# A hybrid decoder layer on one Trainium2 core: keys and queries transposed in squares by VectorE and over DRAM, the taps of a block redistributed, the first products' order and one sum changed

## The reference, cut to what matters

```python
z = h @ w_in                                   # 2048 -> 12288 columns: q, k, v, u, ga and gc, 2048 each
q, k, v, u, ga, gc = jnp.split(z, list(np.cumsum(IN_SPLITS)[:-1]), axis=-1)
# 16 heads of 128: scores = q k^T * scale - slope * distance, causal, softmax, times v
y_attn = o.transpose(0, 2, 1, 3).reshape(B, S, ATTN_WIDTH) @ w_attn_out
# u: a * sigmoid(g), a depthwise convolution with 31 taps over 1024 channels, norm, silu, product
merged = jax.nn.sigmoid(ga) * y_attn + jax.nn.sigmoid(gc) * y_conv
return merged @ w_out
```

## Time and profile before

| | |
|---|---|
| time, median of 3 runs | 2117.32 us (2117.2 to 2117.87) |
| the profiled execution's own time | 2117.16 us |
| its span | 2115.3 us |
| TensorE busy | 2102.1 us (99%) |
| VectorE busy | 1868.6 us (88%) |
| ScalarE busy | 1406.2 us (66%) |
| POOL busy | 194.2 us (9%) |
| HBM | 529.93 MB read, 16.78 MB written |

### The profile page before, as it was taken

The page is one execution under the profiler, slowest core; times in us unless marked ns, Lnnn a source line. Parts: engine busy times, 40 slices in busy tenths (PEclk is TensorE's granted clock), DMA queues, the critical chain, the costliest instruction groups (busy, mean ns, idle before and its releaser), DMA issues.

```text
span 2115.3 us, 23794 instructions
## 1 busy us (share of the span) xinstructions
PE 2102.1 (99%) x9420; PEld 1740.6 (82%) x9420; DVE 1868.6 (88%) x1404; ACT 1406.2 (66%) x1321; POOL 194.2 (9%) x305
## 2 busy tenths in 40 slices
PE   9999999999999999999999999999999999999998
PEld 7888888888888888888888888888888888888886
DVE  8899999999997889999899986659899999999996
ACT  6677777778775547666676435435677777777773
POOL 0111111100110000000000000000111111110110
PEclk9999999999999999999999999999999999999999
DMA  9688888898886759787888656755688888898883
GB/s 359 238 285 274 266 268 269 293 308 277 288 276 237 274 154 316 251 261 224 273 266 251 232 189 231 259 187 199 237 289 262 276 262 275 290 308 276 288 276 123
DMA packets 89709, 548.26 MB, mean 259 GB/s; under 512 B 12416, under 2 KB 12800, under 8 KB 32512
## 3 DMA queue, kind: packets, MB, share of 16 engines
q1 hardware_dynamic: 68544, 437.69, 54.5%
q0 software_dynamic: 21056, 109.07, 24.5%
HBM read 529.93 MB, written 16.78 MB: 258 GB/s over the span
## 4 chain that ended last, share of the span: by engine, by line
PE 99%; DMA 0%; DVE 0%; SPq 0%; ACT 0%; issue 0%; DVEq 0%
PE acc L2194 16%; PE acc L2196 16%; PE acc L2195 16%; PE tb L2194 12%; PE tb L2196 12%; PE tb L2195 12%; PE acc L2132 3%; PE acc L2134 3%; PE acc L2133 3%; PE tb L2180 1%; DMA g_raw<-in_groups 0%; PE tb L2475 0%; PE tb L2491 0%; PE tb L2492 0%; PE tb L2474 0%; DVE res L2035 0%
## 5 line engine op out<-in xcount | busy, mean ns | idle before, releaser
L1326 DVE TENSOR_TENSOR g_lo<-g_raw,g_hi 128x2048 fp32r<-128x2048 f32 x506 | 1147.3, 2285 | 136.5 <-ACT g_hi L804 136.1
L804 ACT ACTIVATE g_hi<-g_raw 128x2048 fp32r<-128x2048 f32 x506 | 964.7, 1916 | 343.3 <-DVE g_raw L1334 105.4
L2194 PE MATMUL acc<-g_hi,xF_hi 128*128 128x512 f32 x1216 | 477.9, 393 | 1.9 <-DVE g_lo L1653 1.3
L2196 PE MATMUL acc<-g_hi,xF_lo 128*128 128x512 f32 x1216 | 473.7, 390 | 0.0
L2195 PE MATMUL acc<-g_lo,xF_hi 128*128 128x512 f32 x1216 | 473.2, 389 | 0.0
L2194 PE MATMUL tb<-g_hi,xF_hi 128*128 128x512 f32 x760 | 297.1, 391 | 0.0
L2196 PE MATMUL tb<-g_hi,xF_lo 128*128 128x512 f32 x760 | 295.9, 389 | 0.0
L2195 PE MATMUL tb<-g_lo,xF_hi 128*128 128x512 f32 x760 | 295.7, 389 | 0.0
L1334 DVE TENSOR_TENSOR g_raw<-g_raw,g_raw 128x2048 f32<-128x2048 f32 x120 | 274.3, 2286 | 1.4
L2194 PEld LDWEIGHTS acc<-g_hi,xF_hi 128*128 128x128 f32 x1216 | 228.3, 188 | 50.3 <-DVE g_lo L1653 2.6
L2196 PEld LDWEIGHTS acc<-g_hi,xF_lo 128*128 128x128 f32 x1216 | 228.3, 188 | 48.2
(11 more groups left out here) (169 smaller groups left out, 2243.5 us busy)
## 6 DMA issues: line engine op xcount, KB each, us to landing
g_raw<-in_groups SPq DMA_DIRECT2D x356, 1024.0 KB, 7.0
g_raw<-in_groups POOLq DMA_DIRECT2D x80, 1024.0 KB, 8.3
raw<-in_stream SPq DMA_DIRECT2D x80, 512.0 KB, 4.7
bounce<-h_sq POOLq DMA_DIRECT2D x40, 256.0 KB, 5.0
h_in<-bounce POOLq DMA_DIRECT2D x160, 64.0 KB, 2.8
ln_gb<-in_ln SPq DMA_DIRECT2D x6, 1024.0 KB, 6.9
g_raw<-in_groups SPq DMA_DIRECT2D x6, 512.0 KB, 9.1
res<-in_x_rows SPq DMA_DIRECT2D x1, 2048.0 KB, 16.0
```

Of the source, the lines that this page charges most:

```text
L804: act.activation(g_hi[:, n % RING], source[:], ACT.Copy).then_inc(g_hi_ready, 1)
L1326: dve.tensor_tensor(g_lo[:, n % RING], source[:], f32(g_hi[:, n % RING]), ALU.subtract).then_inc(g_lo_ready, 1)
L2194: pe.matmul(bank, x_hi_ap, g_hi[:, n % RING, blk], start=begin, stop=False, skip_group_check=True)
L2196: return pe.matmul(bank, x_lo_ap, g_hi[:, n % RING, blk], start=False, stop=end, skip_group_check=True)
```

## The change

Five edits:

1. The key and query transposes leave TensorE. VectorE transposes 32x32 squares of both (four passes per head block), POOL stores them to two new DRAM buffers and loads them back in 16 pieces, ScalarE copies the queries into `qT`; the keys are loaded straight into `kT`, in another order of the tokens' addresses, which the scores' products read with strides (`tokens`). ScalarE no longer copies keys.
2. TensorE makes the first pair's scores behind P5a (before: ahead of it) and the second pair's behind P6a (before: ahead of it).
3. `BLOCK_TAPS` has ten numbers per block. Head blocks have none in the first four places and 2 or 3 in the others; the gate chunks get one more per group.
4. In `first_chunk` TensorE runs the two kinds of products that need only `g_hi` first and those with `g_lo` behind them; `WARM` is 10.
5. In the first feed-forward part the sum T3 of block 1 is made by POOL's adding DMA, and two low halves of x factors (`factor_lo(f, 2)`, `(f, 3)`) move behind T1.

```diff
-WARM = 12
+WARM = 10
...
-BLOCK_TAPS = ((1, 3), (1, 3), (1, 3), (1, 3), (2, 3), (2, 1))
+HEAD_TAPS = (0, 0, 0, 0, 2, 2, 3, 3, 3, 3)
+BLOCK_TAPS = ((3, 3, 1, 1, 3, 1, 1, 1, 1, 1), *([HEAD_TAPS] * NG), (1, 1, 2, 2, 1, 2, 2, 2, 2, 2))
...
-            def heads_of(dst, g, first):
-
-                for t in range(TT):
-                    act.wait_ge(tr_full, turned(g) + first + t + 1)
-                    act.activation(dst[:, :, t * P:(t + 1) * P], tb[:, t].rearrange("p (b n) -> p b n", b=HG),
-                                   ACT.Copy).then_inc(qk_ready, 1)
...
             def queries_turned(g):
+
+                act.wait_ge(q_loaded, 16 * TT * QD * (g + 1))
                 if g:
                     act.wait_ge(o_stored, 16 * g)
-                heads_of(qT, g, 2)
+                for t in range(TT):
+                    act.activation(qT[:, :, t * P:(t + 1) * P].rearrange("p b (a n) -> p a b n", a=QD), q_sq[t][:],
+                                   ACT.Copy).then_inc(qT_ready, 1)
...
-                if heads:
-                    keys_turned(g - 1)
-                elif g == 0:
+                if g == 0:
                     conv_block(1)
                 fork(f, g, acc[:, BY], acc[:, BX], "P1b")
                 act.wait_ge(t1b_ready, fulls(f, g))
                 split(f, g, "P5b", "qb")
+                split_sum(f, g, "P6a", "qa", "T2a")
                 if heads:
                     queries_turned(g - 1)
-                split_sum(f, g, "P6a", "qa", "T2a")
...
-                load_done(f, b, "ua")
-                dve.wait_ge(t_ready, G.sum_no[f, b, "T1"])
-                add(ra, ra, ua)
+                if f:
...
+                else:
+                    factor_lo(f, 2)
+                    factor_lo(f, 3)
+                    load_done(f, b, "ua")
...
+            def square(dst, src, squared_one):
+
+                dve.transpose(dst.rearrange("p c b n -> p b c n"),
+                              src.rearrange("p (b c n) -> p b c n", b=BLK, c=QD)).then_inc(squared_one, 1)
...
                 lo_group(f, g, "P1b", "qb")
+                if heads:
+                    keys_squared(g - 1)
                 split_done(f, g, "P1a")
                 load_done(f, g, "ra")
                 add(qa, qa, ra)
                 lo_group(f, g, "Q1", "Q1")
...
-                taps(some)
+                if heads:
+                    queries_squared(g - 1)
+                taps(counts[0])
...
-                taps(5 if g - 1 in HEADS_AT else 7)
+                taps(6 if g - 1 in HEADS_AT else 8)
...
+            def squares_out(g, squared_one, squares, dram, sent):
+
+                for t in range(TT):
+                    pool.wait_ge(squared_one, 2 * g + t + 1)
+                    pool.dma_start(dram[t].rearrange("a p c b n -> (a p) (c b n)"),
+                                   squares[t].rearrange("p c b n -> p (c b n)")).then_inc(sent[t], 16)
+
+            def heads_in(g, sent, dst, dram, loaded_all):
+
+                for t in range(TT):
+                    pool.wait_ge(sent[t], 16 * (g + 1))
+                    for c in range(QD):
+                        pool.dma_start(dst[t][STEP * c:STEP * (c + 1)].rearrange("p a b n -> p a (b n)"),
+                                       dram[t, :, :, c].rearrange("a p b n -> p a (b n)")).then_inc(loaded_all, 16)
...
+            pool.wait_ge(t_ready, G.sum_no[0, 1, "T1"])
+            add_from_hbm(0, 1, "ra", "ua", t3_first)
             round_trips(0)
...
                 for h, (g, first, last) in enumerate(PARTS):
                     p = g // 2
-                    pe.wait_ge(part_lo, h + 1)
+                    pe.wait_ge(part_hi, h + 1)
...
+                    for t in range(TT):
+                        for blk in range(first, last):
+                            high_only(banks[g % 2][t], piece(p, t)[0][:, blk], g, blk, p == 0 and blk == 0)
...
+                    pe.wait_ge(part_lo, h + 1)
+                    for t in range(TT):
+                        for blk in range(first, last):
+                            mm = high_low(banks[g % 2][t], piece(p, t)[0][:, blk], g, blk)
...
-                if heads:
-                    turn_k(g - 1)
...
-                if heads:
-                    turn_q(g - 1)
                 query_group(g, 1)
-                if heads:
-                    scores(g - 1, 0)
...
                 product_group(f, g, "P5a", W, S1, 0, begin=True)
+                if heads:
+                    scores(g - 1, 0)
                 product_group(f, g, "P5b", W, S1, 1)
+                wait_fork(f, g, 0)
+                product_group(f, g, "P6a", X, S2, 0)
                 if heads:
                     scores(g - 1, 1)
-                wait_fork(f, g, 0)
-                product_group(f, g, "P6a", X, S2, 0)
```

More of the change, by code:

```diff
@@ L154, in __init__ @@
                     rows += 1
-                for name in FULL_SUMS if is_full(b) else HALF_SUMS:
+                for name in FULL_SUMS if is_full(b) else HALF_SUMS[f]:
                     sums += 1
@@ L431, in build @@
         t1b_ready = sem("t1b_ready")
+        t3_first = sem("t3_first")
         t3b_ready = sem("t3b_ready")
@@ L475, in build @@
         conv_step = sem("conv_step")
-        qk_ready = sem("qk_ready")
+        k_squared = sem("k_squared")
+        q_squared = sem("q_squared")
+        k_sent = [sem(f"k_sent{t}") for t in range(TT)]
+        q_sent = [sem(f"q_sent{t}") for t in range(TT)]
+        kT_loaded = sem("kT_loaded")
+        q_loaded = sem("q_loaded")
+        qT_ready = sem("qT_ready")
         s_ready = sem("s_ready")
@@ L1810, in mixing_block @@
                 qa, qb, ra, ua, ub = (source(f, g, name) for name in ("qa", "qb", "ra", "ua", "ub"))
-                few, some = BLOCK_TAPS[g]
+                counts = BLOCK_TAPS[g]
                 heads = 0 < g <= NG
@@ L1829, in mixing_block @@
                 add(qa, qa, ua)
-                taps(some)
+                taps(counts[1])
                 lo_group(f, g, "P5b", "qb")
@@ L1850, in mixing_block @@
                     normalised(g - 1)
-                taps(some)
+                taps(counts[4])
                 lo_group(f, g, "P4a", "qa")
-                taps(few)
+                taps(counts[5])
                 lo_group(f, g, "P2a", "ga")
-                taps(few)
+                taps(counts[6])
                 lo_group(f, g, "P2b", "gb")
-                taps(few)
+                taps(counts[7])
                 lo_group(f, g, "P4b", "qb")
-                taps(few)
+                taps(counts[8])
                 lo_group(f, g, "Q4", "Q4")
                 values(g)
-                taps(few)
+                taps(counts[9])
             taps_done = [0]
@@ L2100, in mixing_sums @@
                 add_from_hbm(f, g, "qb", "rb", t1b_ready)
+                if 0 < g <= NG:
+                    squares_out(g - 1, k_squared, [kT[:, t] for t in range(TT)], k_bounce, k_sent)
+                    squares_out(g - 1, q_squared, [tile[:] for tile in q_sq], q_bounce, q_sent)
+                    heads_in(g - 1, k_sent, [kT[:, t] for t in range(TT)], k_bounce, kT_loaded)
+                    heads_in(g - 1, q_sent, [tile[:] for tile in q_sq], q_bounce, q_loaded)
                 k = G.load_at[f, g, "rb"]
@@ L2244, in plain_chunk, with high_only, high_low @@
                                     after[(2 * p + half, t)]()
+            def high_only(bank, x_ap, n, blk, begin):
+                pe.matmul(bank, x_ap, g_hi[:, n % RING, blk], start=begin, stop=False, skip_group_check=True)
+            def high_low(bank, x_ap, n, blk):
+                return pe.matmul(bank, x_ap, g_lo[:, n % RING, blk], start=False, stop=False, skip_group_check=True)
             def first_chunk():
@@ L2253, in first_chunk @@
                     p = g // 2
-                    pe.wait_ge(part_lo, h + 1)
+                    pe.wait_ge(part_hi, h + 1)
+                    if h in (0, 4, 6):
+                        pe.wait_ge(x_hi, (0, 4, 6).index(h) + 1)
+                    for t in range(TT):
+                        for blk in range(first, last):
+                            high_only(banks[g % 2][t], piece(p, t)[0][:, blk], g, blk, p == 0 and blk == 0)
                     if h in (0, 4, 6):
@@ L2258, in first_chunk @@
                         for blk in range(first, last):
-                            mm = mm3(banks[g % 2][t], piece(p, t)[0][:, blk], piece(p, t)[1][:, blk], g, blk,
-                                     p == 0 and blk == 0, False)
+                            high_only(banks[g % 2][t], piece(p, t)[1][:, blk], g, blk, False)
+                    pe.wait_ge(part_lo, h + 1)
+                    for t in range(TT):
+                        for blk in range(first, last):
+                            mm = high_low(banks[g % 2][t], piece(p, t)[0][:, blk], g, blk)
                     if last == GK:
```

69 lines of the change are left out of this document (39 added, 30 removed).

## The result

| | before | changed |
|---|---|---|
| time, median of 4 runs | 2117.35 us (2117.20 to 2117.87) | 2150.66 us (2149.73 to 2152.24) |
| the profiled execution's own time | 2117.16 us | 2149.73 us |
| its span | 2115.3 us | 2147.9 us |
| TensorE busy | 2102.1 us | 2103.7 us |
| POOL busy | 194.2 us | 240.6 us |

The ratio is 1.0157, with an interval of 1.0141 to 1.0173: slower, by 33.3 us or 1.6%. The forecast was 2112.2, its range ended at 2126.0.

The account below looks back on a forecast made before the run. TensorE's list was taken to bound the kernel: 2117.16 - 7.0 (transposes) - 1.2 (first products) + 2.8 (trip over DRAM) + 0.4 (VectorE's squares) = 2112.2 us, range 2108.5 to 2126.

Parts of the forecast that it names:

- The way over DRAM: Head blocks: queries' trip by POOL and DMA ends 0.7 us after the scores are due, 2.8 us back over four blocks.
- I take the best rows: Trip over DRAM: choice of the profile's best stall and landing times, giving 0.7 us late per block.
- T1b's landing before the first load: Sign named for the head blocks: POOL's sum T1b lands before the first key load.
- the keys sent at +6.5: Trip's start: keys stored to DRAM 6.5 us after the block's first product; +7.9 at worst.
- The middling values: Trip over DRAM with 6.3 us for a lot and 2.8 to land: about 4.9 us late per block.
- Rival (b): Head blocks: the trip sets the block, 4.9 us late each, 19.6 back, 2129 us in all; chance 0.25.
- Transposes off TensorE: Head blocks: two lots of eight transposes at 0.87 us leave TensorE in four blocks, 7.0 us less.
- Squares on VectorE: Head blocks: four transposes, 2.6 to 2.8 us, fit on VectorE; no lead at P3b, 0.4 us in all.
- First products: Kernel's start: fifth part begins at about 12.4 instead of 13.63, 1.2 us less, and u1 without a wait.
- Taps: Nine more in each head block's second part, eight in the gate chunks: costs nothing, or 1 us if lead runs out.

Follow-up runs that it names:

- experiment 2: Changed kernel with 30 products of no use on TensorE ahead of each head block's first scores, in the gap of the wait: 2143.78 us.
- experiments 7 and 9: 7: changed kernel with the sum T1b cut to one row of 128 in the four head blocks, 2147.37 us; 9: the run act_loads, 2122.39 us.
- act_loads: Changed kernel with the queries' eight loads issued by ScalarE on its own queue instead of by POOL: 2122.39 us, ratio 1.0023.
- first_alone: Kernel before with edits 4 and 5 alone (first products, WARM, T3 by POOL), transposes staying on TensorE: 2116.35 us, ratio 0.9995.
- keys_final: Changed kernel, but queries transposed on TensorE; T3a before T3b in last head block, taps moved, attention rows sooner, third ones in two parts: 2111.98 us, ratio 0.9974.
- act_mended: act_loads with T3a ahead of T3b in the last head block, five taps per head block ahead of the second biases, attention rows sooner: 2120.42 us.
- experiment 4: Changed kernel with the gate chunks' taps as before and seven more taps in the last head block: 2149.19 us.
- k_trip_first: Changed kernel with the keys' stores and their eight loads all issued by POOL ahead of the sum T1b: 2158.71 us.

## Why the prediction was wrong

With what was measured, its own sum reads 2117.16 - 7.0 - 1.2 + 30.0 + 9.2 + 1.4 = 2149.6; the profiled execution took 2149.73. The 9.2 is what the blocks' lengths left over, so that the sum closes proves nothing by itself; experiment 2 is what ties it to the clock.

- **The way over DRAM failed, at "I take the best rows".** The forecast was 0.7 us late per block, the measured value 7.5. T1b's landing before the first load and the keys sent at +6.5 were right, and so were little over 2 us for the queries' loads, though these fell on +17.6 to +25 and not on +12 to +18. Wrong was the keys' lot: I took 0.91 us for its stall and had in mind the stretch from 845.70 with the DMA share at 0.14, where the queries' loads were to fall. (Even +12 to +18 was half outside it: from 842.80 to 848.80 the share was 0.43.) The keys' fell on +6 to +15, where the share was 0.98 before any edit. They landed in 7.1 us instead of 2.1, POOL stalled 6.8 us on them, and the queries' loads, quick in themselves, stood behind. The middling values, 4.9 us, were nearer, and they too were low.
- **A term was missing: the clock.** Each wait of 2.7 us and more was followed by products at the lower level; at 4.5 us and more it cost some 2 us each time, and even about 2 us of wait could do it. The sum priced a wait at its length, in every rival. Rival (b) was the one that came, with the right place and sign, and put 19.6 on it where 39.2 were measured.
- **The best value was chosen for a wait that all depends on.** The prediction itself said that three of its numbers were the best of their rows, and a rule of the Trainium skill (page "VectorE: DVE Perf Modes", section "Rules for kernel authors"), that such a transpose belongs on TensorE, stood against it. For the queries and keys together the rule held in every run; for the keys alone it did not, once the waits behind were mended. As to the cause, experiments 7 and 9 give the effect of each alone, which need not add: T1b's 1 MB 1 us a block, the queries' loads in POOL's queue 6. The Trainium skill, page "DMA: Bandwidth & Descriptors", section "Rules for kernel authors", says that spreading transfers over issuing engines adds no bandwidth and saves only issue time. The first half agrees (over a block's first 15 us the engines moved 298 GB/s with the loads on ScalarE's queue and 297 without). The time saved was no trifle here: 28.3 us, since with the issues went POOL's stalls and the place behind the keys.
- **Transposes off TensorE:** right. No run gives the 7.0 by itself, but in act_loads, where the clock stayed up, the first blocks took 66.9 us less their waits where they took 68.5 before, and for the keys alone the spans of first_alone and keys_final differ by 3.1 us where 3.5 is the sum, with the waits at both nearly alike.
- **Squares on VectorE:** right for the kernel as it is (no wait for a low half in the head blocks), and as tight as forecast: the five taps of act_mended made P3b 0.8 late.
- **First products:** right, 1.2 us in the trace of the changed kernel and between the medians of first_alone, whose interval still holds no change. In the other runs with this start P1a of the first head block began between 828.88 and 829.75, 1.0 to 1.9 us sooner than before. u1 had no wait.
- **Taps:** "nothing" was off by 1.4 us, at the output products, beyond the gate chunks where I had looked. Half of it is the taps; the other half stays open, behind a high half of ScalarE's (experiment 4).
- **Slips that changed nothing:** by its own terms the range up to 2126 takes in 4.2 us of lateness a block, not 3.4. The taps added to the second part of a head block are eight in three blocks and three in the last, not nine.

## What to carry to other kernels

A share or a landing time has to be read in the stretch where each transfer will fall, one stretch for every lot, since the lots of one queue add up. Where an engine that bounds the kernel may wait, price the wait at its length and add what its clock costs behind it; here the first 1.9 us cost no more than themselves, 5 us did. When a trip is late, try another engine's queue as well as another order, and halve the edit: here the half with the keys was in time and worth keeping.

## What had not been expected of the hardware

- POOL's issue of a load stalls, it seems while too much of what it has issued has not landed: one to four stalls per lot of 512 KB, in eight transfers or four, up to 6.7 us long (k_trip_first, last head block). A lot in a quiet stretch had one of 1.9 to 2.1 us. ScalarE's queue took the same eight with no stall, in 4.2 us. That it goes by what has not landed fits all of this and is not proven.
- TensorE's clock fell in waits of 4.5 us and more (0.50 behind one of 7.5), fell also in one of 2.7 (0.61 behind it) and in four of six of about 2 us, and did not in those of up to 1.90. Products without a use kept it at 1.00 and made the kernel 6.9 us faster.
